# One diffusion step with a 32-expert mixture: weights laid out per partition, token rows fetched from DRAM by index

## The reference, cut to what matters

```python
g_top, g_idx = lax.top_k(softmax(h @ rg_w + rg_b), 1)       # one of 4 groups
# top 2 of the group's 8 experts, weights from their logits
hid = silu(x_blk @ w1[e]) * (x_blk @ w3[e])                 # 1024 -> 512, twice
y[token] += slot_w * (hid @ w2[e])                          # 512 -> 1024
```

## Time and profile before

| what | value |
|---|---|
| device time, median of 3 (least to most) | 2256.29 us (2256.17 to 2258.19) |
| span of the profiled execution, first to last instruction | 2252.2 us |
| PE busy | 1994.3 us, 89% |
| DVE, ACT, POOL busy | 644.7, 397.6, 125.0 us |
| moved by DMA | 506.15 MB, mean 225 GB/s |
| mean granted TensorE clock | 0.962 |
| first up-projection of layer 1's and layer 2's expert stage | at 560.57 and 1666.39 us |

### The profile page before, as it was taken

How to read it: one execution, slowest core, us unless ns; L and a number is a source line. 1 busy time by engine, 2 the same in 40 slices (tenths; PEclk the granted TensorE clock), 3 DMA queues, 4 the chain that set the end, 5 groups by cost and what they waited for, 6 DMA issues and landing times. The chain is left out here.

```text
span 2252.2 us, 27802 instructions
## 1 busy us (share of the span) xinstructions
PE 1994.3 (89%) x11050; PEld 1206.9 (54%) x11050; DVE 644.7 (29%) x1495; ACT 397.6 (18%) x785; POOL 125.0 (6%) x200
## 2 busy tenths in 40 slices
PE   6999788987999999999679997889879999999994
PEld 3556577765445444444345665677554554444442
DVE  3034566543011011110122437664521111111012
ACT  1022343213101011011011223341211101101001
POOL 0002012200000000000000111122000000000000
PEclk8999999997999999999899999999979999999997
DMA  9661000023999999999687410000359999999992
GB/s 299 213 205 38 15 1 1 15 72 134 393 379 360 368 355 364 365 362 364 245 267 225 131 47 1 1 1 27 138 198 394 363 364 361 368 358 363 367 357 112
DMA packets 256452, 506.15 MB, mean 225 GB/s; under 512 B 5104, under 2 KB 84976, under 8 KB 255984
## 3 DMA queue, kind: packets, MB, share of 16 engines
q1 hardware_dynamic: 254208, 502.98, 62.3%
q10 hardware_dynamic: 2160, 2.03, 0.3%
HBM read 502.90 MB, written 2.10 MB: 224 GB/s over the span
## 5 line engine op out<-in xcount | busy, mean ns | idle before, releaser
L1557 PE MATMUL bank<-arena 128*64 128x512 f32 x2048 | 447.0, 594 | 0.0
L1557 PEld LDWEIGHTS bank<-arena 128*64 128x64 f32 x2048 | 143.5, 136 | 279.2 <-issue 275.3
L1572 PE MATMUL bank<-arena 128*64 128x512 f32 x1024 | 226.8, 595 | 22.5 <-ACT arena L1668 20.8
L477 PE MATMUL bank<-arena 128*128 128x385 f32 x704 | 237.1, 493 | 3.7 <-ACT arena L897 3.7
L1535 PE MATMUL bank<-arena 128*128 128x128 f32 x1536 | 191.4, 282 | 45.4 <-DVE arena L1652 23.7
L1535 PEld LDWEIGHTS bank<-arena 128*128 128x128 f32 x1536 | 179.9, 195 | 78.7 <-DVE arena L1652 50.2
L477 PEld LDWEIGHTS bank<-arena 128*128 128x128 f32 x704 | 133.7, 193 | 93.0 <-issue 7.5
L1564 PE MATMUL bank<-arena 128*128 128x384 f32 (+2 forms) x768 | 174.9, 384 | 1.7 <-DVE arena L1652 1.7
L858 POOL TENSOR_TENSOR arena<-arena,const 128x256 f32<-128x256 f32 x168 | 122.9, 755 | 759.1 <-DVE arena L1213 593.2
L1564 PEld LDWEIGHTS bank<-arena 128*128 128x128 f32 x768 | 123.3, 190 | 59.8 <-issue 27.8
L1572 PEld LDWEIGHTS bank<-arena 128*64 128x64 f32 x1024 | 71.6, 135 | 155.7 <-issue 129.0
(11 more groups left out here) (246 smaller groups left out, 1868.5 us busy)
## 6 DMA issues: line engine op xcount, KB each, us to landing
arena<-in_exp_w SPq DMA_DIRECT2D x198, 2048.0 KB, 13.3
arena<-in_w_mod SPq DMA_DIRECT2D x48, 1024.0 KB, 6.5
arena<-in_w_in SPq DMA_DIRECT2D x22, 1024.0 KB, 9.9
arena<-in_w_out SPq DMA_DIRECT2D x8, 768.0 KB, 4.4
const<-in_const SPq DMA_DIRECT2D x1, 2213.5 KB, 11.0
arena<-in_w_out SPq DMA_DIRECT2D x2, 1024.0 KB, 4.9
x_sb<-in_xT SPq DMA_DIRECT2D x1, 1536.0 KB, 6.4
out_yT<-arena SPq DMA_DIRECT2D x1, 1536.0 KB, 5.1
```

What stands on the lines that cost most here:

```text
L477: last = mm(b[:, 0:W - 2], w[:, c, j * P:(j + 1) * P], hT[:, c, 1:W - 1], start=(c == 0), stop=(c == KC - 1))
L1557: last = mm(b[HALF[j], :], Xg[:, c, j, :], unit[2 * m + j][:, c * DE:(c + 1) * DE], start=(c == 0), stop=(c == KC - 1))
L1572: last = mm(b[HALF[j], :], hidT[:, f_, j, :], unit[4 + j][:, lo:lo + 512], start=(f_ == 0), stop=(f_ == FC - 1))
```

## The change

All large weight arrays are laid out on the host so that one load is one contiguous run a partition (`pieces`): w1, w3 and w2 of an expert become 128 rows of 16 KB, the pieces of w_mod and w_in 128 rows of 8 KB, those of w_out 6 KB with its last two chunks as an array of their own. The loads lose their `(c p)` rearrangement; buffers, order and waits of SP stay.

The gathers inside the loop go. At the end of the mixer SP stores `h2tok` to a DRAM tensor `h2_rows`, a row for each token. In the up-projection of pair i, PE multiplies `Sel` of pair i+1 by a column of token numbers (`tokid`), which gives the token of each of the 128 slots (0 where a slot is empty) in one column of `bB`; DVE turns it into integers; POOL issues an indirect DMA that brings the 128 rows of 4 KB into `xtok`; PE transposes four blocks of them in the place of each gather (`turned`). Pair 0 still uses the two selection matmuls. `bB` is now handed over five times a pair (`B_IN_PAIR`).

```diff
+        slot_tok = sb("slot_tok", 1, I32)
+        h2_rows = nc.dram_tensor("h2_rows", (T, D), F32, kind="Internal").ap()
...
+        xtok = moe(D)
...
-                        sp.dma_start(stream[n % 2] if dst is None else dst, src.rearrange("(c p) n -> p c n", p=P))\
+                        dst = stream[n % 2] if dst is None else dst
+                        sp.dma_start(dst, src.rearrange("p (c n) -> p c n", c=dst.shape[1]))\
                           .then_inc(sem(f"piece_loaded{n % 2}"), 16)
...
                         sp.dma_start(mod_stream[n % 2],
-                                     a["w_mod"][rows, n * UC:(n + 1) * UC].rearrange("(c p) n -> p c n", p=P))\
+                                     a["w_mod"][bass.ds(layer * (N_MOD * P) + n * P, P), :]
+                                     .rearrange("p (c n) -> p c n", c=KC))\
                           .then_inc(sem(f"mod_loaded{n % 2}"), 16)
...
+                    pr.copied(sp, f"htok{TILES - 1}1")
+                    sp.dma_start(h2_rows.rearrange("(t p) d -> p t d", p=P), h2tok).then_inc(sem("h2_stored"), 16)
                     sp.wait_ge(sem("stored"), 48)
                     sp.wait_ge(sem("first_loaded"), 48)
+                    sp.wait_ge(sem("h2_stored"), 16)
...
-            IN_PAIR = 4
+            IN_PAIR, B_IN_PAIR = 4, 5
...
-                        name, rows = (("exp_w1", D), ("exp_w3", D), ("exp_w2", DE))[m]
-                        src = a[name][bass.ds((layer * N_EXP + i * 2 + j) * rows, rows), :]
-                        sp.dma_start(unit[2 * m + j].rearrange("p (c n) -> p c n", c=rows // P),
-                                     src.rearrange("(c p) n -> p c n", p=P)).then_inc(sem(f"unit{2 * m + j}"), 16)
+                        src = a[("exp_w1", "exp_w3", "exp_w2")[m]][bass.ds((layer * N_EXP + i * 2 + j) * P, P), :]
+                        sp.dma_start(unit[2 * m + j], src).then_inc(sem(f"unit{2 * m + j}"), 16)
...
+                    def slot_tokens():
+                        for t in range(TILES):
+                            last = mm(bB[:, 0:1], Sel[:, t, :, :].rearrange(js), ck("tokid", 1, t),
+                                      start=(t == 0), stop=(t == TILES - 1))
+                        last.then_inc(sem("b_filled"), 1)
+
+                    def turned(half):
+                        b = bB if half else bA
+                        for c in range(4):
+                            last = nc.tensor.transpose(b[:, c * P:(c + 1) * P],
+                                                       xtok[:, (4 * half + c) * P:(4 * half + c + 1) * P], ident)
+                        last.then_inc(sem("b_filled" if half else "a_filled"), 1)
...
                                 if c == 4 and not m:
                                     emptied_b(pe, i, 0)
+                                    if not last_pair:
+                                        pe.wait_ge(sem("sel_ready"), i + 2)
+                                        slot_tokens()
...
                         if not last_pair:
-                            pe.wait_ge(sem("sel_ready"), i + 2)
-                            gather(0)
+                            pe.wait_ge(sem("rows_gathered"), i * 16 + 16)
+                            turned(0)
...
                             emptied_b(pe, i, B_DOWN)
-                            gather(1)
+                            turned(1)
...
-                        full_b(dve, i, B_UP)
+                            full_b(dve, i, B_IDX)
+                            v.tensor_copy(slot_tok[:, :], bB[:, 0:1]).then_inc(sem("b_emptied"), 1)
+                        full_b(dve, i, LAST_UP if last_pair else B_UP)
...
+                @block.gpsimd
+                def _(pool):
+                    for i in range(LAST):
+                        emptied_b(pool, i, B_IDX)
+                        nc.gpsimd.indirect_dma_start(xtok, None, h2_rows[:, :],
+                                                     bass.IndirectOffsetOnAxis(ap=slot_tok[:, 0:1], axis=0))\
+                            .then_inc(sem("rows_gathered"), 16)
+                    pool.wait_ge(sem("rows_gathered"), 16 * LAST)
+                    pool.dma_reset()
...
+    def pieces(x, n):
+        c = x.shape[-2] // P
+        x = x.reshape(-1, c, P, x.shape[-1] // n, n).transpose(0, 3, 2, 1, 4)
+        return np.ascontiguousarray(x.reshape(-1, c * n))
```

More of the change, by code:

```diff
@@ L63 @@
                   ("cos", TS), ("sin", TS), ("att", 2 * P), ("tri", 4 * P), ("level", 2 * LEVELS * P),
-                  ("reset", 3 * 129), ("iota", SLOTS), ("rev", EPG), ("eps", 2)):
+                  ("reset", 3 * 129), ("iota", SLOTS), ("rev", EPG), ("eps", 2), ("tokid", TILES)):
     CK[_name] = _n
@@ L790, in load_mod @@
                         sp.dma_start(mod_stream[n % 2],
-                                     a["w_mod"][rows, n * UC:(n + 1) * UC].rearrange("(c p) n -> p c n", p=P))\
+                                     a["w_mod"][bass.ds(layer * (N_MOD * P) + n * P, P), :]
+                                     .rearrange("p (c n) -> p c n", c=KC))\
                           .then_inc(sem(f"mod_loaded{n % 2}"), 16)
-                    rows = bass.ds(layer * D, D)
                     for n in range(N_MOD1):
@@ L797, in _ @@
                     for m, u in enumerate(IN_ORDER):
-                        load(m, a["w_in"][rows, u * UC:(u + 1) * UC])
+                        load(m, a["w_in"][bass.ds(layer * (N_IN * P) + u * P, P), :])
                         for n in MOD_WITH[m]:
@@ L802, in _ @@
                     for u in range(N_OUT):
-                        load(N_IN + u, a["w_out"][bass.ds(layer * D, 6 * P), u * UC:(u + 1) * UC],
+                        load(N_IN + u, a["w_out"][bass.ds(layer * (N_OUT * P) + u * P, P), :],
                              stream[(N_IN + u) % 2][:, 0:6, :])
-                    load(N_IN + N_OUT, a["w_out"][bass.ds(layer * D + 6 * P, 2 * P), :],
+                    load(N_IN + N_OUT, a["w_out_rw"][bass.ds(layer * P, P), :],
                          stream[(N_IN + N_OUT) % 2].rearrange("p c n -> p (c n)").rearrange("p (c n) -> p c n", c=2))
@@ L809, in _ @@
                     for j in range(2):
-                        sp.dma_start(unit[j].rearrange("p (c n) -> p c n", c=KC),
-                                     a["exp_w1"][bass.ds((layer * N_EXP + j) * D, D), :]
-                                     .rearrange("(c p) n -> p c n", p=P)).then_inc(sem("first_loaded"), 16)
+                        sp.dma_start(unit[j], a["exp_w1"][bass.ds((layer * N_EXP + j) * P, P), :])\
+                          .then_inc(sem("first_loaded"), 16)
                     pr.filled(sp, f"out1_{KC - 1}")
-                    sp.dma_start(unit[2].rearrange("p (c n) -> p c n", c=KC),
-                                 a["exp_w3"][bass.ds(layer * N_EXP * D, D), :].rearrange("(c p) n -> p c n", p=P))\
+                    sp.dma_start(unit[2], a["exp_w3"][bass.ds(layer * N_EXP * P, P), :])\
                       .then_inc(sem("first_loaded"), 16)
@@ L1460, in experts_round @@
         def experts_round(layer):
-            IN_PAIR = 4
+            IN_PAIR, B_IN_PAIR = 4, 5
             A_UP, A_WT, A_TOK, A_DOWN = 1, 2, 3, 4
-            B_UP, B_HT, B_DOWN, B_TOK = 1, 2, 3, 4
+            B_IDX, B_UP, B_HT, B_DOWN, B_TOK = 1, 2, 3, 4, 5
+            LAST_UP, LAST_HT, LAST_DOWN = 1, 2, 3
             LAST = PAIRS - 1
@@ L1483, in full_b @@
                 def full_b(eng, i, k):
-                    eng.wait_ge(sem("b_filled"), i * IN_PAIR + (k + 1))
+                    eng.wait_ge(sem("b_filled"), i * B_IN_PAIR + (k + 1))
                 def emptied_a(eng, i, k):
@@ L1489, in emptied_b @@
                 def emptied_b(eng, i, k):
-                    eng.wait_ge(sem("b_emptied"), i * IN_PAIR + (k + 1))
+                    eng.wait_ge(sem("b_emptied"), i * B_IN_PAIR + (k + 1))
                 def pairs(eng, body):
@@ L1520, in _ @@
                         load(0, 0, j)
-                    full_b(sp, LAST, B_UP)
+                    full_b(sp, LAST, LAST_UP)
                     load(0, 1, 0)
@@ L1544, in loaded, with up @@
                             pe.wait_ge(sem(f"unit{2 * m + j}"), i * 16)
-                    def up(i):
+                    def up(i, last_pair):
                         emptied_a(pe, i, 0)
@@ L1551, in up @@
                             if m:
-                                emptied_b(pe, i, 0)
+                                emptied_b(pe, i, 0 if last_pair else B_IDX)
                             for c in range(KC):
@@ L1582, in rest @@
                         last.then_inc(sem("a_filled"), 1)
-                        emptied_b(pe, i, B_UP)
+                        emptied_b(pe, i, LAST_UP if last_pair else B_UP)
                         for f_ in range(FC):
@@ L1604, in _ @@
                     gather(1)
-                    up(0)
+                    up(0, False)
                     rest(0, False)
                     with pe.Fori(1, LAST) as i:
```

(15 more changed lines are left out.)

2 lines of the change are left out of this document (1 added, 1 removed).

## The result

| | before | after |
|---|---|---|
| device time, median (least to most) | 2256.23 us (2255.62 to 2258.19) | 2143.12 us (2142.32 to 2144.53) |
| span of the profiled execution | 2252.2 us | 2140.6 us |
| one expert pair, up-projection to up-projection | 34.74 us | 31.09 us |
| PE's waits for w_mod, both layers | 28.0 us | 20.9 us |
| moved by DMA | 506.15 MB | 525.03 MB |

The ratio is 0.9499, 95% interval [0.9487, 0.9511]: 113 us faster. The forecast was 2137, range 2108 to 2215.

A forecast was written before the change was run, and what follows sets the result against it. PE was taken to bound the expert stage, DMA second by 2.7 us a pair. -116 + 4 - 7.5 = -119.5 on the 2252.2 span gave 2132.7, or 2137 as median; range 2108 to 2215 out to B's case of DMA bound.

The forecast's parts named there:

- Step 1: Expert pair loop: transposes replace the two gathers, saving 2.34 and 2.28 us a pair; stops of 0.69 and 0.79 stay.
- Step 2: Middle of each up-projection: three one-column matmuls, six instructions, add 0.75 us a pair, bounds 0.3 and 1.8.
- the lower bound's 0.05 each: Token numbers in the up-projection: 0.05 us an instruction if a weight load hides behind its neighbours, 0.3 for six.
- the slower row behind the upper one: Token numbers' upper bound of 1.8 us: twice a row where 12 of 32 columns took 1.75, 0.15 each.
- Step 3: Row fetch, from index to first transposes: lands in about 8 us of the 16.7 available, hidden, 8 us to spare.
- Rival D: PE's wait before `turned(0)`: fetch queues behind the load backlog, 7.7 us late, 231 us in all, 2368; chance 0.08.
- Step 4: Expert loads: at 422 GB/s a pair needs 31.1 us of DMA, 0.2 more than PE; 4 us charged in all.
- The lead: Expert loads: issued 23.9 us before use, landing after 13.3; 10 us of slack takes up most of the deficit.
- Rival B: Expert stage: longer runs bring nothing, DMA becomes the bound at 33.4 us a pair, 2196 us; chance 0.16.
- The upper bound of 430: Expert loads' top rate in GB/s, from packets of 85 ns for 2 KB, 160 for 4 KB, 75 each further 2 KB.
- Step 5: Mixer openings, PE's waits for w_mod: contiguous pieces save 7.5 us over two layers, bounds 0 and 18.6.
- Step 6: Mixer's end: store of h2 to DRAM hidden with 1.8 us; POOL's reset at the stage's end also 0.

The follow-up runs named there:

- The two late fetches: Changed kernel with the fetch issued only after ACT took the w1 product, 2165.93 us, or after DVE took the w3 product, 2430.32 us.
- the fetch alone: Changed kernel with the weights row-major as before and the row fetch kept: 2213.59 us, ratio 0.9803 to the kernel before.
- the layout is worth 6 us alone: Kernel before with contiguous weights only, the gathers staying selection matmuls: 2251.18 us, ratio 0.9973 to the kernel before.
- the pair of 30.72 us with it and 29.57 without: Changed kernel with both transposes moved into the scatter, 2132.01 us; the same with only the first of a stage's 15 fetches issued, 2099.47 us.

## Why the prediction was right, step by step

**Step 1, the gathers.** From the first transposes to the down-projection it is 823.82 - 822.48 = 1.34 us in the pair shown (1.29 forecast), and from the second ones to the next up-projection 832.39 - 831.71 = 0.68 (0.60). The two stops stayed, as forecast.

**Step 2, the token numbers.** The up-projection went from 13.90 us to 816.11 - 801.30 = 14.81: 0.91, where 0.75 was taken. In the timeline the six are busy for 0.83 us, 0.14 each; the lower bound's 0.05 each is in no row, and the slower row behind the upper one, the twelve of the earlier trace rows, ran at a granted clock of 0.82. These 0.16 and the 0.13 of step 1 are a little more than the 0.22 between a pair of 30.87 and one of 31.09 us. 30 x 3.65 = 109.5 us instead of 116; measured from the first up-projection to DVE's last step of the stage, each layer's stage is 54.6 us shorter.

**Step 3, the fetch.** Hidden, as forecast, but landing in 10.8 us instead of 8, with 5.5 us to spare instead of 8.7. That it held in pair 0, which the prediction didn't look at, was luck: at 10.8 us it would have had 0.6 us to spare there, and it has 5.2 because few loads stand beside it (1.5 load packets an engine, against 7.6). The two late fetches show that this was the step with the steepest price: beyond the spare time, more than one for one. Rival D named the right place, PE's wait before `turned(0)`, and the wrong reason: the fetch doesn't stand behind the backlog, since it lands in 7.6 us where loads take 19.6 and in 10.8 where they take 14.6. The packet records show how: by single runs, 8 packets of the fetch among 7.6 of the loads in the change, 614 ns each at the median, and among 8.8 in the fetch alone, where those of 4 KB take 164 ns. Beside the longer packets the fetch's own 8 take 5.9 us, beside the shorter ones 2.7.

**Step 4, the loads.** 426 GB/s against 422, DMA's floor 30.72 us a pair against 31.1, which is under PE's 31.09. So there was no deficit, and the 4 us charged for one were not spent. The lead that was to cover most of it was not needed, and where loads do fall short, in the fetch alone, it covers little: the second pair is already at their pace. That the layout is worth 6 us alone, the fetch 43 and both 113 is this step: each moves one of two bounds that lay 2.7 us apart. Rival B was what the fetch alone does: 33.21 us a pair, for the 33.4 worked out. The upper bound of 430 and the 1.28 us of the fetch were estimates from 385 and 409 GB/s, which on one of 16 engines are 85 ns for 2 KB and 160 for 4 KB. The packet records of the kernel before have 86 and 159 ns at the median, and the changed kernel's of 16 KB have 614, where 160 and six times 75 make 610. The fetch's 128 packets are 8 an engine, 1.27 us at 159 ns; the pair of 30.72 us with it and 29.57 without shows at least 1.15.

**Step 5, the openings.** 28.0 us of waits for w_mod became 20.9: 7.1 for 7.5. PE's waits for DMA in the first opening, and in the second:

```profile
PE bank L428 <- DMA arena<-in_w_mod: 15.5, 7, 9.8
```

```profile
PE bank L428 <- DMA arena<-in_w_mod: 5.4, 5, 1.9
```

The first matmul of w_in comes at 48.2 instead of 51.4, and in layer 2 the way from the stage's end to it is 3.9 us shorter: 7.1 again, by a measure that doesn't depend on what a wait is put down to.

**Step 6, the store and the reset.** Nothing, as forecast. PE stands idle for 14.63 us after the first stage, where the reset would show, and for 14.48 in the kernel before. SP's waits at the end of the first mixer: 4.9 us for the store, and after it another 2.5 for PE at the block's end.

```profile
SPq L833 <- DMA h_rows<-arena: 4.9, 1, 4.9
SPq L410 <- PEq L410: 2.5, 1, 2.5
```

**What the sum missed.** 109.2 for the stages and 7.1 for the openings make 116.3, and the span is 111.6 us shorter. The other 4.7 are spread over stretches in which the change was given no cost: the two ways from router to first up-projection 1.0 us longer each, layer 2's mixer 2.9 longer and layer 1's 0.8 shorter, the end 0.5. In the first of these the granted clock is 0.58 (the third window of the profile after) instead of 0.63, with the same 49 matmuls. In the kernel before:

```profile
546.81:560.57 13.76, 7.39 (x49) 7.27 (x49) 0.70 (x4) 3.16 (x3) 0.00 (x0) 0.63 0.47 154
```

Why the clock differs there was not tried, and the cause of the 4.7 us stays open. On the span the forecast was 2132.7 and 2140.6 came: 2.8 less for the stages than the 112 forecast, 0.4 less for the openings, and these 4.7.

## What to carry to other kernels

Before costing a cut on the engine that sets the pace, work out the second bound in the same unit, here the loads of a pair at the rate measured while they queue: a gain ends where the second bound lies, and an edit that is worth nothing alone may be what lets another one pay. Give every asynchronous fetch its deadline in each form of the loop body, the first and last included. And treat a stall of PE of several microseconds as dearer than its length: behind waits of 4.9 and 6.6 us the granted clock was 0.70 and 0.68 over the next 11.7 us, while the stops of 0.7 and 0.8 us in each pair left the granted clock at 1.00.

## What the runs showed of the hardware that had not been expected

- Load rates rise with the length of the run in a partition, and go on rising above 4 KB: 385 GB/s at 2 KB, 409 at 4 KB, 426 at 16 KB, the last held for whole pairs while PE worked.
- A row fetch from GpSimd (128 rows of 4 KB) occupied POOL for 0.94 us; its landing went from 7.6 to 10.8 us with the length of the packets beside it, and was 6.0 to 6.2 where few loads stood beside it.
- A wait of 6.6 us on PE cost 9.7: the granted clock was 0.68 in the 11.7 us behind it.
